# Five of six modulation groups summed over k on VectorE inside the merge stages of a two-layer diffusion backbone

## The reference

```
for l in range(2):
    mod   = silu(c)     @ w_mod[l] + b_mod[l]          # w_mod[l]: 1024 x 6144
    mod_c = silu(c_ctx) @ w_mod[l] + b_mod[l]
    sh1, sc1, gt1, sh2, sc2, gt2 = split(mod, 6)       # the same for mod_c
    h = rmsnorm(x, g_pre1) * (1 + sc1) + sh1           # hc from the context
    y, y_c = token_mixers(h, hc, ...)                  # MLA + neighbourhood attention + mLSTM
        # ends in merge: y = (g_a*(a @ w_br_mla) + g_b*(b @ w_br_na) + g_m*(m @ w_br_ml)) @ w_out
        # with g_a, g_b, g_m = sigmoid of 3 x 1024 gate columns of h @ w_in
    x = x + gt1 * rmsnorm(y, g_post1)
    h2 = rmsnorm(x, g_pre2) * (1 + sc2) + sh2
    x = x + gt2 * rmsnorm(expert_choice_ffn(h2, w_router, w_e1, w_e3, w_e2), g_post2)
    # layer 0 does the same for the context; layer 1 needs no context output
```

## Time and profile before

| | us |
|---|---|
| runs | 2041.23, 2047.76, 2048.48 (median 2047.76) |
| the profiled execution | 2042.77, span 2041.0 |
| PE / DVE / ACT / POOL busy in the span | 1730.0 / 468.3 / 317.0 / 86.7 |
| merge of layer 0 | 366.88 to 571.04 |
| merge of layer 1 | 1400.46 to 1490.5 |

### The profile page before, as it was taken

One profiled execution on the slowest core, in us unless ns is written; L12 is line 12 of the kernel. 1 busy time (PEld: TensorE's weight loads), 2 busy tenths in 40 slices (PEclk: granted clock), 3 DMA queues, 4 the chain that ended last, 5 costly groups with the idle time before them and its releaser, 6 DMA issues.

```text
span 2041.0 us, 21556 instructions
## 1 busy us (share of the span) xinstructions
PE 1730.0 (85%) x9237; PEld 882.1 (43%) x9237; DVE 468.3 (23%) x972; ACT 317.0 (16%) x742; POOL 86.7 (4%) x138
## 2 busy tenths in 40 slices
PE   5999999999997998989888699999977667667655
PEld 1656444444475432423222266757863223223222
DVE  2145044211115111202111514253122101011102
ACT  2113144100023010001000311242020000000001
POOL 4000110000002100000000000110000000000000
PEclk8999999999999999999999899999997777776877
DMA  9310104454416799999999932114634999999996
GB/s 348 95 42 21 16 1 186 169 183 167 164 63 260 319 421 421 421 421 421 421 421 421 389 96 62 16 36 150 206 124 188 421 421 421 421 420 420 421 421 257
DMA packets 130666, 525.15 MB, mean 257 GB/s; under 512 B 9886, under 2 KB 73532, under 8 KB 75276
## 3 DMA queue, kind: packets, MB, share of 16 engines
q1 hardware_dynamic: 127884, 520.47, 64.4%
q0 software_dynamic: 2688, 3.32, 0.9%
HBM read 522.70 MB, written 1.05 MB: 257 GB/s over the span
## 4 chain that ended last, share of the span: by engine, by line
PE 56%; DMA 37%; DVE 5%; ACT 1%; issue 1%; SPq 0%; DVEq 0%; ACTq 0%
DMA ring<-in_w_e_dram 35%; PE ps L645 13%; PE ps L893 9%; PE ps L1038 6%; PE ps L899 4%; PE ps L929 4%; PE ps L857 3%; PE ps L585 2%; PE ps L819 2%; PE ps L991 2%; PE ps L1060 2%; PE ps L735 2%; PE ps L1018 1%; DMA ring<-in_w_mod_dram 1%; PE ps L591 1%; PE ps L841 1%
## 5 line engine op out<-in xcount | busy, mean ns | idle before, releaser
L1038 PE MATMUL ps<-ring,arena 128*32 128x256 f32 (+1 forms) x3072 | 408.4, 510 | 135.5 <-DMA ring<-in_w_e_dram 132.1
L1038 PEld LDWEIGHTS ps<-ring,arena 128*32 128x32 f32 (+1 forms) x3072 | 131.3, 129 | 396.2 <-DMA ring<-in_w_e_dram 221.8
L1060 PE MATMUL ps<-ring,arena 128*32 128x256 f32 (+1 forms) x1536 | 224.2, 567 | 82.2 <-DMA ring<-in_w_e_dram 78.7
L893 PE MATMUL ps<-arena,ring 128*128 128x512 f32 (+1 forms) x576 | 192.4, 487 | 0.0
L645 PE MATMUL ps<-arena,ring 128*128 128x512 f32 (+1 forms) x480 | 176.9, 527 | 1.4 <-DVE arena L1522 1.4
L1060 PEld LDWEIGHTS ps<-ring,arena 128*32 128x32 f32 (+1 forms) x1536 | 70.9, 142 | 231.9 <-DMA ring<-in_w_e_dram 114.0
L1360 ACT ACTIVATE arena<-ps 128x512 f32<-128x512 f32 (+1 forms) x32 | 15.7, 491 | 831.3 <-PE ps L1038 831.3
L893 PEld LDWEIGHTS ps<-arena,ring 128*128 128x128 f32 x576 | 108.7, 190 | 77.9 <-issue 70.4
L1707 DVE COPY arena<-ps 32x512 f32<-32x512 f32 (+1 forms) x128 | 70.9, 554 | 284.8 <-PE ps L1060 283.5
L645 PEld LDWEIGHTS ps<-arena,ring 128*128 128x128 f32 x480 | 90.8, 191 | 83.6 <-issue 77.7
L1700 DVE TENSOR_TENSOR arena<-arena,ps 128x512 f32<-128x512 f32 (+1 forms) x32 | 17.7, 554 | 386.9 <-PE ps L1038 386.9
(11 more groups left out here) (185 smaller groups left out, 1292.4 us busy)
## 6 DMA issues: line engine op xcount, KB each, us to landing
ring<-in_w_e_dram SPq DMA_DIRECT2D x384, 1024.0 KB, 17.9
ring<-in_w_mod_dram SPq DMA_DIRECT2D x48, 1024.0 KB, 9.1
ring<-in_w_in_dram SPq DMA_DIRECT2D x44, 1024.0 KB, 10.5
ring<-in_w_out_dram SPq DMA_DIRECT2D x8, 1024.0 KB, 10.3
arena<-in_w_br_ml_dram SPq DMA_DIRECT2D x8, 512.0 KB, 6.5
arena<-in_w_br_mla_dram SPq DMA_DIRECT2D x8, 256.0 KB, 3.9
arena<-in_w_br_na_dram SPq DMA_DIRECT2D x8, 256.0 KB, 4.8
arena<-in_rpb_dram POOLq DMA_DIRECT2D x16, 96.0 KB, 4.1
```

Source lines behind the costliest of these rows:

```text
L893: mm = pe.matmul(ps[:, u % 3, tq], wg[:, k, cols], hT[:, k, tq], start=k == 0, stop=k == KD - 1)
L1038: mm = pe.matmul(ps[M * j:M * j + M, m, 0:NW], XST[e // GROUP % 2][:, kk, e % GROUP, 0:M], w[:, k, j * NW:(j + 1) * NW], start=kk == 0, st ...
L1060: mm = pe.matmul(ps[M * j:M * j + M, 3, 0:NW], lhs, w[:, k, j * NW:(j + 1) * NW], start=kk == 0, stop=kk == KD - 1)
```

## The change

For groups 1 to 5 VectorE multiplies each slot by `cT[:, k, s]`, a scalar for each partition, and adds it to an accumulator of 2048 columns, once per stream s (both in layer 0, only the latent one in layer 1): `mod_part`. The partitions are then added by TensorE with a stationary matrix `pick` that has ones in one column: `mod_sum`, 4 matmuls per stream. Groups 1, 2 and 3 stay in layer 0's merge, at units 0 to 6, 8 to 14 and 16 to 22; groups 4 and 5 move to layer 1's merge, at units 0 to 7 and 9 to 16. Their loads move with them. TensorE gives the slots back, at every odd unit, and waits for VectorE's `mod_part` before it.

```diff
+MERGE_GROUPS = [(1, 2, 3), (4, 5)]
+GROUP_UNITS = [8, 9]
+def merge_mods(l, u):
+    i, at = divmod(u, GROUP_UNITS[l])
+    if i >= len(MERGE_GROUPS[l]):
+        return []
+    o = MERGE_GROUPS[l][i]
+    if l:
+        return [(o, at)] if at < KD else []
+    return [(o, k) for k in range(KD) if at == max(k - 1, 0)]
+def sum_unit(l, o):
+    return GROUP_UNITS[l] * (MERGE_GROUPS[l].index(o) + 1) - 1
 def weight_loads(layer):
-    loads = [("mod", *MOD_GROUPS[5 if layer else 0], k) for k in range(KD)]
+    loads = [] if layer else [("mod", *MOD_GROUPS[0], k) for k in range(KD)]
...
-            if layer == 0:
-                loads += [("mod", *MOD_GROUPS[1 + n // KD], n % KD) for n in mod_steps(3 * jp + m)]
+            for u in (6 * jp + 2 * m - 1, 6 * jp + 2 * m):
+                if u >= 0:
+                    loads += [("mod", *MOD_GROUPS[o], k) for o, k in merge_mods(layer, u)]
...
-    if layer == 0:
-        loads += [("mod", *MOD_GROUPS[4], k) for k in range(KD)]
...
+            def mods_done(l, u):
+                mods = merge_mods(l, u - 2) + merge_mods(l, u - 1) if u > 1 else merge_mods(l, 0)
+                if mods:
+                    o, k = mods[-1]
+                    pe.wait_ge(sem("mod_part"), KD * (o - 1) + k + 1)
+                taken[0] += len(mods)
+                return len(mods)
+            def mod_sum(l, o):
+                pe.wait_ge(sem("mod_part"), KD * o)
+                pe.wait_ge(sem("mod_row"), o)
+                for s in ([1] if l else [0, 1]):
+                    for j in range(4):
+                        acc = mod_acc[1][:, 2 * j:2 * j + 2, :] if l else mod_acc[0][s][j]
+                        dst = ps[32 * j:32 * j + 32, 6, :]
...
+                        mm = pe.matmul(dst, pick[:, s, :], acc, start=l == 1 or s == 0, stop=s == 1, skip_group_check=True)
+                mm.then_inc(sem("mod_summed"), 1)
+            def merge_unit_end(l, u):
+                for o in MERGE_GROUPS[l]:
+                    if u == sum_unit(l, o):
+                        mod_sum(l, o)
+                    if u == sum_unit(l, o) + 2:
+                        mod_turn(o)
...
                             for k in range(nk_):
+                                if k == nk_ - 2 and half:
+                                    freed = (1 if jp else 0) + mods_done(l, u)
                                 mm = pe.matmul(ps[:, 3 + u % 3, tq], wb[:, k0 + k, cols], src[:, k, tq],
                                                start=k == 0, stop=k == nk_ - 1)
-                                if k == 0 and jp and half:
-                                    mm.then_inc(used, 1)
+                                if freed and k == nk_ - 2:
+                                    mm.then_inc(used, freed)
                             mm.then_inc(sem("mg_branch"), 1)
+                            merge_unit_end(l, u)
                             u += 1
-                        if l == 0:
-                            merge_mods(3 * jp + m)
...
-                else:
-                    for k in range(KD):
-                        mod_product(5, k)
                 norm_turn(l, 1, xn1, range(4))
-                if l:
-                    mod_turn(5)
...
-                if l == 0:
-                    pe.wait_ge(sem("g1_taken"), 4)
-                    for k in range(KD):
-                        mod_product(4, k)
...
+            def mod_part(l, o, k):
...
+                if l:
+                    pieces = [(1, mod_acc[1], w_slot(n).rearrange("p (a n) -> p a n", a=KD))]
+                else:
+                    a, b = mod_acc[0]
+                    pieces = [(1, view(18432, SLOT), w_slot(n)), (0, view(20992, 1536), w_slot(n)[:, 0:1536]),
+                              (0, a[3], w_slot(n)[:, 1536:SLOT])]
+                for s, acc, w in pieces:
+                    if k:
+                        ins = dve.scalar_tensor_tensor(out=acc, in0=w, scalar=cT[:, k, s:s + 1], in1=acc,
+                                                       op0=ALU.mult, op1=ALU.add)
+                    else:
+                        ins = dve.tensor_scalar(acc, w, cT[:, k, s:s + 1], None, ALU.mult)
+                ins.then_inc(sem("mod_part"), 1)
...
                         else:
                             own(ins)
+                    for o in MERGE_GROUPS[l]:
+                        if u == sum_unit(l, o) + 1:
                             mod_row(o)
+                    for o, k in merge_mods(l, u):
+                        mod_part(l, o, k)
```

More of the change, by code:

```diff
@@ L49 @@
 MOD_GROUPS = [(l, g) for l in range(2) for g in range(3)]
-MERGE_STEPS = 3 * KD // 2
+MERGE_UNITS = 3 * KD
+MERGE_GROUPS = [(1, 2, 3), (4, 5)]
+GROUP_UNITS = [8, 9]
 def rope_table():
@@ L240, in backbone @@
         one_add = sb("one_add", 3)
+        pick = sb("pick", 2, 32)
         eps_t = sb("eps_t", 1)
@@ L243, in backbone @@
         top8 = sb("top8", 8)
-        ARENA = 23568
+        ARENA = 24080
         arena = sb("arena", ARENA)
@@ L298, in backbone @@
         tmp_m = view(20480, T)
+        mod_acc = {0: [[view(at, 512) for at in (20992, 21504, 22016, 23568)],
+                       [view(18432 + 512 * j, 512) for j in range(4)]],
+                   1: view(4096, KD, T)[:, :, 0:CTX]}
         Ym = view(14336, 4, D)
@@ L470, in _ @@
             own(pool.memset(wrt[:, :, :], 0.0))
+            own(pool.memset(pick[:, :, :], 0.0))
+            for s in range(2):
+                pool.memset(pick[:, s, s:s + 1], 1.0)
             pool.memset(cT[:, :, :], 0.0)
@@ L553, in _ @@
                 if l == 0:
-                    mod_rows(5)
                     params(1)
@@ L570, in _ @@
                     rel_bias(1)
+                    mod_rows(5)
         @block.tensor
@@ L593, in mod_product @@
                 mm.then_inc(used, 1)
[L595 to L603, removed]
+            def mods_done(l, u):
[13 more added lines that the diff above has]
+                        if l:
+                            dst = dst.rearrange("p (a n) -> p a n", a=2)
+                        mm = pe.matmul(dst, pick[:, s, :], acc, start=l == 1 or s == 0, stop=s == 1, skip_group_check=True)
[5 more added lines that the diff above has]
+                    if u == sum_unit(l, o) + 2:
                         mod_turn(o)
@@ L962, in _ @@
                 mm.then_inc(sem("logits"), 1)
-                if l == 0:
-                    mod_turn(4)
                 R = N_EXP * L.ns
@@ L1295, in _ @@
                     act.activation(sg_m[u % 3][:, tq], src[:, tq], ACT.Sigmoid).then_inc(sem("mg_sig"), 1)
-                    for o in range(1, 4):
-                        if l == 0 and u % 2 and mod_step(o) == u // 2 - 1:
+                    for o in MERGE_GROUPS[l]:
+                        if u == sum_unit(l, o) + 3:
                             mod_cols(o)
@@ L1390, in mod_row @@
                 dst = mod_tmp[:, :] if g == 0 else gate_rows[:, 2 * l + g - 1, :]
-                dve.wait_ge(used, mod_loaded(o))
+                if o:
+                    dve.wait_ge(sem("mod_summed"), o)
+                else:
+                    dve.wait_ge(used, KD)
                 dve.wait_ge(sem("mod_rows_ready"), o + 1)
@@ L1395, in mod_row @@
                                          op0=ALU.add, op1=ALU.mult).then_inc(sem("mod_row"), 1)
+            def mod_part(l, o, k):
+                n = BASE[l] + ring_loads(l).index(("mod", *MOD_GROUPS[o], k))
+                done_ = KD * (o - 1) + k
+                dve.wait_ge(landed[n % SLOTS], 16 * uses(n))
+                if done_:
+                    dve.wait_ge(sem("mod_part"), done_)
+                if k == 0 and o > 1:
+                    dve.wait_ge(sem("mod_summed"), o - 1)
+                if l:
+                    pieces = [(1, mod_acc[1], w_slot(n).rearrange("p (a n) -> p a n", a=KD))]
[7 more added lines that the diff above has]
+                                                       op0=ALU.mult, op1=ALU.add)
+                    else:
+                        ins = dve.tensor_scalar(acc, w, cT[:, k, s:s + 1], None, ALU.mult)
+                ins.then_inc(sem("mod_part"), 1)
             def norm_rows(l, which, j, t, dst):
@@ L1420, in _ @@
                     dve.wait_ge(sem("mod_col"), 1)
-                else:
-                    mod_row(5)
                 norm_lat(l, 1, hT)
@@ L1607, in _ @@
                             own(ins)
-                    for o in range(1, 4):
-                        if l == 0 and u % 2 and mod_step(o) == u // 2:
+                    for o in MERGE_GROUPS[l]:
+                        if u == sum_unit(l, o) + 1:
                             mod_row(o)
+                    for o, k in merge_mods(l, u):
+                        mod_part(l, o, k)
+                if l == 0:
+                    mod_row(3)
                 def post(which, j, t, Y, G, tmp):
@@ L1628, in _ @@
                 norm_lat(l, 2, h2T)
-                if l == 0:
-                    mod_row(4)
                 ns = L.ns
```

10 lines of the change are left out of this document (1 added, 9 removed).

## The result

The changed kernel takes 2083.61 us (median of 4 runs, 2082.78 to 2084.37) against 2045.76 for the kernel before (median of 4 runs): a ratio of 1.0194 with a 95% interval of 1.0176 to 1.0211. It is slower by 1.9%, and the whole interval lies above 1. The forecast was 2087, in a range of 2066 to 2106.

The account below looks back on a forecast made before the run. TensorE, gapless in both merges, was taken to bound the kernel, with merge delays passed on in full. Terms 16.0 + 7 + 15 + 1 + 3 - 0.7 = +41 gave 2084 or 2089 us; it took 2087, range 2066 to 2106.

Parts of the forecast that it names:

- a delay is passed on in full: Both merges: TensorE sets the experts' start and their 192 loads the length, so any merge gain or loss reaches the end.
- Removed and added work on TensorE: Layer 0's merge: twelve product pairs go (24.6 us), three mod_sum come (6.2), net -18.4 us if TensorE never waits.
- The walk through the first six units: Layer 0's merge: the units end at 41.4 us against 13.7 of TensorE's own work, so 27.7 us of waiting.
- The waits as a whole: TensorE's waits for VectorE: 27.7 us in layer 0's first six units, then 4.2 and 2.5; in layer 1 11.8.
- One of the signs: Sign to look for: L1433 on VectorE stands in layer 0's merge chain for about 28 to 35 us up to unit 5.
- The clock: TensorE's granted clock falls when it rests: +7 us in layer 0's merge, +1 in layer 1's, +3 at 635 to 640.
- +3 at norm 2: At 635 to 640 us, without group 4's products, transposes and the router's product run colder: +3 us (0 to 5).
- Layer 1's merge: No products removed; +11.8 us of waits in the first six units, +3.1 of sums and turns: +15, plus 1 of clock.
- (a): Multiply-adds run at the tensor_scalar's rate, a k of both streams is 2.85 us: about +13 us, 2060; 5 in 100.
- (b): TensorE never really waits, as VectorE has 174 us free: -16 us, about 2029; 4 in 100.
- (c): Without group 4's 8 loads ahead of them, the experts begin 20 us sooner: +41 - 20, 2067; 6 in 100.
- (d): The transfers of layer 1's merge run dry: +10 us, 2097; 12 in 100.

Follow-up runs that it names:

- late start: Against the changed kernel, layer 0's 24 sums over k begin at unit 5, where units are longer; layer 1 unchanged: 2044.99 us, ratio 1.0014 to the kernel before.
- busy waits: The changed kernel plus 9, 11 and 8 unused matmuls ahead of the waits of units 1, 3 and 5 in layer 0's merge: 2080.61 us.
- layer-0-only kernel: Against the changed kernel, groups 4 and 5 are TensorE products at their old places again; groups 1 to 3 stay on VectorE: 2064.77 us.
- late start in both: Against the changed kernel, all five groups' sums on VectorE begin at unit 5 in both merges: 2031.33 us, ratio 0.9944 to the kernel before.
- half the sum: Against the changed kernel, the context stream's sums in layer 0 are left out (its modulation is wrong), all waits stay: 2064.38 us.
- the later give-back: Against the changed kernel, TensorE gives the modulation slots back two units later, with the same work on every engine: 2050.33 us.
- late start with later slots: Against the changed kernel, groups 4 and 5 are TensorE products again, groups 1 to 3 sum from unit 5, slots return two units later: 2031.92 us.
- layer-1-only kernel: Against the changed kernel, groups 1 to 3 are TensorE products between the units again; groups 4 and 5 stay on VectorE: 2062.83 us.

## Why the prediction was right, step by step

**The place.** The forecast put +39 us into the two merges and +2.3 elsewhere; +42.1 are there and -1.9 elsewhere, +40.2 by the profiles for a forecast +41. That the sum is so close is in part luck: the merges came out 3 us too low and the rest 4 too high. That a delay is passed on in full held, since the experts' stages kept their length (727.9 to 727.5, 484.6 to 484.1). The first of these stretches holds group 5's turn, for which -0.7 was forecast.

**Removed and added work on TensorE.** -24.6 + 6.2 = -18.4. In the late start, where nothing waits, the merge is 186.3: 204.1 - 18.4 = 185.7. The term was right to 0.6 us.

**The walk through the first six units.** It had 41.4 us at full clock and 46.4 with the clock's 5. Unit 6's gates start at 45.5; with the clock kept up at 406.61 - 366.24 = 40.4. It was 1 us high. Five k are 4.76 us each and not 5.0, and k = 0 is 2.54 and not 2.85, which is 1.5 us less; three pairs of matmuls behind a pause take 1.97 even at full clock and not 1.72, which is 0.7 more. (A k is less than the sum of its durations, 2.35 + 1.81 + 0.75 = 4.91, because they overlap a little.) The Trainium skill, "VectorE: DVE Perf Modes", section "The TRN2 errata — SBUF-src ops pay a fixed extra latency per instruction", has 2.19 us for 2048 elements (58 cycles and one an element at 0.96 GHz, an estimate by that page); measured were 2.35. The same section of the Trainium skill adds that its 58 cycles come out too low and that some 150 were measured for a copy; by those the estimate is 2.29, which the prediction passed over.

**The waits as a whole.** Five waits were forecast in layer 0, five there are. In all they are 30.5 us, forecast 34.4. In the first six units it is 24.5 for 27.7: 1 us is the walk's excess above, and 2.2 are TensorE's own work, which at half clock takes up part of each wait. At units 9 and 17 it is 3.7 and 2.3 for 4.2 and 2.5: there the prediction's own terms (1.5 + 1.44 + 2.85 + 5.0) sum to 10.8 and not to the 11.1 that it used. The 6.6 us that it gives for VectorE's products in the first six units should be 7.1; the walk doesn't use it. In layer 1 it was 9.7 for 11.8. One of the signs was off: L1433 stands in the chain for about 24 us up to unit 5 (five k), not 28 to 35.

**The clock.** Forecast +7 in layer 0, +1 in layer 1, +3 at norm 2. The +7 was 5 for the pairs and 2 for a cold unit 6. The pairs paid 5.1 (shown by the busy waits), but unit 6 started warm: its gates took the usual 6.87 us. What the prediction put at nothing is the clock behind the later waits: the pairs of units 9 and 17 took 3.75 and 3.04 us, and unit 10's gates 7.41, in all some 4 us, which no run isolates:

```profile
450.03 3.75 PE ps L930 x4
453.78 0.85 PE ps L601 x4
454.63 7.41 PE ps L921 x16
...
533.38 3.04 PE ps L930 x4
```

So layer 0's total (+23.9 for a forecast +23) is that close partly by luck. The waits were 3.9 us too high. TensorE's own work is 11.7 us more than in the late start, which does the same work (197.3 against 185.6 us busy), where the clock was given 7; 2.2 of these are the half-clock work inside the waits. In layer 1 the clock was under 1.00 from 1431 to 1447 us (0.55 at 1435 to 1439), and waits and clock together came to 13.9 in the first six units, where 12.8 was forecast. The +3 at norm 2 was wrong: that stretch measures +0.1. The clock did fall to 0.50 there (660 to 665 us), but it was back at 1.00 by 670. And before the change the transposes, which begin at 640.68, had run at 0.66 in any case; the prediction's row ended at 640. The first row is of before, the others of after:

```profile
640.00:645.00 5.00, 4.23 (x20) 3.41 (x21) 2.71 (x5) 2.26 (x4) 0.00 (x0) 0.66 1.01 426
660.00:665.00 5.00, 0.81 (x4) 0.84 (x5) 4.05 (x2) 0.64 (x4) 5.00 (x4) 0.50 0.08 13
665.00:670.00 5.00, 4.61 (x28) 3.52 (x27) 3.36 (x7) 3.46 (x7) 1.57 (x3) 0.78 0.47 131
670.00:675.00 5.00, 3.40 (x28) 1.64 (x26) 1.14 (x3) 1.61 (x3) 0.00 (x0) 1.00 0.01 3
```

**Layer 1's merge.** +18.2 for a forecast +16. The added TensorE work is 3.3 in the chain (two sums of 1.0, 0.2 more on the gates behind each, two turns of 0.46), 3.1 forecast. What was missing is 1.1 in the waits and clock of the first six units, 0.6 for unit 6's gates at the end of the half clock, and a short wait at 1490.7 us.

**The rivals.** (a) is out by the 2350 ns of the 2048-element multiply-add; (b) by five waits; (c) by the stretch to the experts, which is 101.7 us without group 4's loads in it, 101.5 before the change and 100.6 in the layer-0-only kernel with them; (d) because no engine waited for a load in layer 1's merge, and by the late start in both.

**What the text didn't say.** The prediction called the waits the consequence of VectorE's work in short units. The runs show that three things have to come together: sums of 4.76 us, in units of 1.7 us, and a give-back that asks for the k of the unit just before. Taking away any one helps: half the sum took 23 us off layer 0's merge, the later give-back 24, and the longer units all of the waits (42). These are no shares of one loss, since they overlap. The walk contains all three, but the text didn't name the place of the give-back, or that of the sums, as what could be had back without less work.

**Open.** The clock's share in layer 1's merge, and at units 9 and 17 of layer 0's, was not measured by itself. The profile of the late start with later slots is its slowest run (2038 of 2028 to 2038), with the stretch from layer 0's experts 6 us longer (733.8); why isn't known. The layer-1-only kernel's merge 1 is 110.2 and not 109.3, from one profile each.

## What to carry to other kernels

An engine that is idle 85% of the time on the average (VectorE in layer 0's merge) can still be the bound: before work is moved to it, walk through the shortest stretch between two hand-overs, not through the mean. If engine A has to report that engine B is done with a buffer, put that report some steps behind, as far as the ring allows (two units took 33 us off here), but give everything back before the next stage's loads need it (5.8 us were lost where that was late). Work that fills an engine's own wait costs nothing, and moving it away buys nothing: the removed products of groups 4 and 5 were such work.

## What the runs showed of the hardware

Keeping TensorE busy with matmuls that nobody uses made the first six units of a stage 5.1 us shorter (45.5 to 40.4), since it kept the granted clock at 1.00 and the two matmuls behind a wait took 1.97 us in place of 3.77. I had expected the clock to cost something, but not that added work pays for itself inside a path that another engine sets.
